# Prompt's dilated attention: copies of turned blocks placed between the exponentials of the next unit, scores issued three units ahead

## The reference, cut to what matters

```python
s = jnp.einsum("znqhe,znkhe->znhqk", qb, kb).astype(jnp.float32) * scale
s = s - slopes[:, None, None] * (dist * dilation).astype(jnp.float32)
s = jnp.where(valid[None, :, None], s, NEG_INF)
m = jnp.max(s, axis=-1)
e = jnp.exp(s - m[..., None])
den = jnp.sum(e, axis=-1)
o = jnp.einsum("znhqk,znkhe->znqhe", e, vb.astype(jnp.float32))
# merge_groups, with M the largest m of the groups:
num = sum(o * jnp.exp(m - M)[..., None] for o, m, _ in parts)
den = sum(dn * jnp.exp(m - M) for _, m, dn in parts)
return num / den[..., None]
```

## Time and profile before

| | us |
|---|---|
| Median of 3 runs | 1567.02 (1566.27 to 1567.53) |
| The profiled execution's own time | 1569.71 |
| Span of the profiled execution | 1567.9 |
| Busy in the span: TensorE / VectorE / GpSimd / ScalarE | 1461.7 / 673.4 / 612.9 / 467.1 |
| First instruction of the stage (line 1043) | at 1068.69 |
| First output-projection product (line 539) | at 1154.34 |

### The profile page before, as it was taken

The page is one execution under the profiler, slowest core; times in us unless marked ns, Lnnn a source line. Parts: engine busy times, 40 slices in busy tenths (PEclk is TensorE's granted clock), DMA queues, the critical chain, the costliest instruction groups (busy, mean ns, idle before and its releaser), DMA issues.

```text
span 1567.9 us, 28214 instructions
## 1 busy us (share of the span) xinstructions
PE 1461.7 (93%) x12103; PEld 1354.0 (86%) x12103; DVE 673.4 (43%) x984; ACT 467.1 (30%) x866; POOL 612.9 (39%) x276
## 2 busy tenths in 40 slices
PE   6969995888999999999999999998879999999998
PEld 6857763555899999999999999887669999999998
DVE  4668776777254400233113454425665420034212
ACT  4215544343332221122322111114633221122322
POOL 1412213342336644466343443231024654366441
PEclk9979997999999999999999999999989999999999
DMA  4234854675243544454433674558923444544421
GB/s 158 76 101 164 296 172 178 243 280 211 84 162 135 194 155 138 154 190 142 154 141 102 215 250 134 171 187 267 315 90 135 144 151 143 205 134 144 151 81 55
DMA packets 124060, 258.80 MB, mean 165 GB/s; under 512 B 7257, under 2 KB 104681, under 8 KB 117697
## 3 DMA queue, kind: packets, MB, share of 16 engines
q1 hardware_dynamic: 117824, 219.73, 41.1%
q0 software_dynamic: 6144, 37.75, 6.5%
HBM read 249.87 MB, written 95.58 MB: 220 GB/s over the span
## 4 chain that ended last, share of the span: by engine, by line
PE 86%; DVE 8%; issue 2%; ACT 2%; another core or an unknown queue 0%; DMA 0%; SPq 0%; POOL 0%; DVEq 0%; ACTq 0%
PE ps L539 23%; PE ps L543 23%; PE ps L540 22%; PE ps L846 4%; PE ps L748 2%; PE ps L867 1%; ACT sc L2276 1%; DVE KT L1566 1%; PE ps L795 1%; PE ps L1051 1%; PE ps L763 1%; PE ps L1085 1%; PE ps L952 1%; PE ps L887 1%; PE ps L728 1%
## 5 line engine op out<-in xcount | busy, mean ns | idle before, releaser
L2328 POOL TENSOR_TENSOR whl<-wraw,whl 128x2048 fp32r<-128x2048 f32 (+3 forms) x127 | 448.6, 3541 | 539.0 <-ACT whl L1975 539.0
L539 PE MATMUL ps<-hA,whl 128*128 128x260 f32 x1216 | 323.4, 287 | 11.1 <-POOL hA L2328 6.0
L540 PE MATMUL ps<-hA,whl 128*128 128x260 f32 x1216 | 318.6, 283 | 0.0
L1975 ACT ACTIVATE whl<-wraw 128x2048 fp32r<-128x2048 f32 (+3 forms) x127 | 186.1, 1486 | 424.6 <-PE ps L543 397.4
L539 PE MATMUL ps<-uT,whl 128*128 128x260 f32 x1024 | 268.4, 283 | 0.0
L540 PE MATMUL ps<-uT,whl 128*128 128x260 f32 x1024 | 266.3, 281 | 0.0
L543 PE MATMUL ps<-hA,whl 128*128 128x260 f32 x1216 | 247.4, 285 | 0.0
L539 PEld LDWEIGHTS ps<-hA,whl 128*128 128x128 f32 x1216 | 231.5, 190 | 14.5 <-issue 12.8
L540 PEld LDWEIGHTS ps<-hA,whl 128*128 128x128 f32 x1216 | 232.0, 191 | 0.1
L543 PE MATMUL ps<-uT,whl 128*128 128x260 f32 x1024 | 206.7, 283 | 0.0
L540 PEld LDWEIGHTS ps<-uT,whl 128*128 128x128 f32 x1024 | 193.2, 189 | 0.0
(11 more groups left out here) (303 smaller groups left out, 1991.9 us busy)
## 6 DMA issues: line engine op xcount, KB each, us to landing
out_ds<-in_state SPq DMA_DIRECT2D x32, 2047.0 KB, 10.4
wraw<-in_w_up SPq DMA_DIRECT2D x32, 1024.0 KB, 5.6
wraw<-in_w_down SPq DMA_DIRECT2D x32, 1024.0 KB, 5.1
wraw<-in_w_qkv SPq DMA_DIRECT2D x18, 1024.0 KB, 5.2
out_ds<-in_state SPq DMA_DIRECT2D x8, 2044.0 KB, 12.3
dv<-in_state SPq DMA_DIRECT2D x36, 256.0 KB, 5.3
dv<-q_scratch SPq DMA_DIRECT2D x6, 1024.0 KB, 6.2
wraw<-in_w_omla SPq DMA_DIRECT2D x4, 1024.0 KB, 11.2
```

Of the source, the lines that this page charges most:

```text
L539: pe.matmul(ps[:, 2 * u + a, 0:HALF], hi(k), rhs(k, 0)[:, c], start=first, stop=False)
L540: pe.matmul(ps[:, 2 * u + a, 0:HALF], hi(k), rhs(k, 1)[:, c], start=False, stop=False)
L1975: ins = act.activation(dst(0), src, ACT.Copy)
L2328: return pool.tensor_tensor(dst, src, hi.bitcast(F32), ALU.subtract)
```

## The change

ScalarE's loop runs one unit longer, and a copy of unit k - 1 follows each quarter of exponentials of unit k. TensorE issues the scores of units 0 to 2 first and then those of unit k + 3 after the second quarter's values of unit k; it also issues the turn of the maxima in unit 6 and the turn of the sums in the first quarter of unit 7, each behind a new wait. VectorE takes the result of a unit out one iteration later. No instruction is added or removed.

```diff
-            d_scores(0)
+            for k in range(3):
+                d_scores(k)
             for k in range(DU):
-                if k + 1 < DU:
-                    d_scores(k + 1)
                 d_turn(k, 0)
-                if k == DU - 1:
-                    for a in range(2):
-                        pe.wait_ge(dil_biased[a], DU)
-                    turn_stats(0, top)
                 for j in range(4):
                     if j < 3:
                         d_turn(k, j + 1)
-                    if k == DU - 1 and j == 2:
+                    if k == DU - 1 and j == 0:
+                        pe.wait_ge(dil_exp, 8 * DU)
                         turn_stats(1, total)
                     d_values(k, j)
+                    if j == 1 and k + 3 < DU:
+                        d_scores(k + 3)
+                    if j == 1 and k == DU - 2:
+                        pe.wait_ge(dil_max_ready, DU)
+                        turn_stats(0, top)
```

```diff
-            for k in range(DU + 2):
+            for k in range(DU + 3):
                 if k < DU:
                     d_max(k)
-                if k == DU + 1:
+                if k == DU + 2:
                     shares()
-                if k >= 2:
-                    d_out(k - 2)
+                if k >= 3:
+                    d_out(k - 3)
```

```diff
-            for k in range(DU):
+            for k in range(DU + 1):
                 for j in range(4):
-                    d_exp(k, j)
-                for j in range(4):
-                    d_taken(k, j)
-                    if k == DU - 1 and j == 2:
-                        share_exp()
+                    if k < DU:
+                        d_exp(k, j)
+                    if k:
+                        d_taken(k - 1, j)
+                if k == DU - 1:
+                    share_exp()
```

## The result

The changed kernel takes 1557.43 us (median of 4 runs, 1555.34 to 1559.50) against 1567.18 us: 9.75 us less, ratio 0.9937 with the 95% interval 0.9923 to 0.9950. The forecast was 1562.3 in a range of 1560.0 to 1566.3. The direction was right and the size was not: the change is worth twice what I said. Its profiled execution took 1557.15 us, with a span of 1555.3.

What follows compares the result with a forecast made beforehand. The stage was taken as bound by a ring of waits through TensorE, ScalarE and VectorE. Units 1 to 7 -7.2 us, tail +1.9, 0.6 taken back for hand-overs and clock: -4.7, median 1562.3, range 1560.0 to 1566.3.

Steps and rivals of the forecast that it cites:

- What bounds the stage: In the 76 us stage no engine is full; links waiting for one another across TensorE, ScalarE and VectorE set the time.
- The ring through three engines: VectorE's bias and maxima, ScalarE's exponentials and copy, TensorE's values and scores, then VectorE again: 17.35 us per pair, floor 14.8.
- the chain of the new order: Unit 1's first exponential to unit 7's, 46.05 us, then 14.3 to the first merge multiply (L1929).
- Even and odd iterations: Middle of the stage, new order: 8.9 us with kind 1 scores, 6.9 with kind 0, so 15.8 a pair against 17.35.
- the one without scores: Iteration 5, which issues no scores: ScalarE paces it, 5.95 us.
- The tail: From unit 7's first exponential to L1929: 14.3 us, 1.9 longer than the 12.4 before, since unit 6's copies are in it.
- The waits behind the new order: VectorE's work stays hidden: slack 1.6 us for scores, 0.5 to 2.6 for exponentials, cost 0 for results taken out later.
- the signs that I had named: Units 1 and 7 46 us apart, pairs 15.8, TensorE over 85% busy, L1929 about 1142.5, clock 1.00 from unit 1 to 6.
- how long the ring takes: Old order, from the first profile: 17.35 us a pair, 53.24 from unit 1's first exponential to unit 7's.
- C: Rival: short pauses drop TensorE's clock to 1.2 GHz in units 5 to 7, costing 7.4 us, giving 1569.7; chance 0.06.
- B: Rival: VectorE late once or twice, or a half-clock stretch stays; gain 2.9 us, 1564.1, down to none; chance 0.13.
- D: Rival: gain given back after the stage, where the projection waits for other engines; late clock costs 1 us; 1566.5; chance 0.05.

Runs made afterwards that it cites:

- warm_start: Changed kernel plus 10 extra identity products in each of TensorE's two waits at the stage's start; ratio 0.9943 to the kernel before.
- scores_two_ahead: Changed kernel with scores issued two units ahead in place of three; 1593.71 us, ratio 1.0145 to the kernel before.
- filler_products: Kernel before plus 7 or 4 extra identity products in TensorE's wait for the first copy of each unit; 1562.14 against 1567.96 us.
- before_again: Kernel before, unedited, profiled and timed once more; ratio 0.9998 to the runs beside it.
- after_again: Changed kernel, unedited, profiled and timed once more; 1559.45 against 1568.25 us for the kernel before, ratio 0.9944.
- after_third: Changed kernel, unedited, run again beside its variants; 1563.41 against 1572.46 us for the kernel before, ratio 0.9943.

## Why the prediction was wrong

- **What bounds the stage**: half of it. The ring through three engines did cost, and the chain of the new order came out at 60.34 us against 60.35 summed; that the clock cost about as much was missed (below). Even and odd iterations took 8.95 and 6.82 us, forecast 8.9 and 6.9; the one without scores 5.88, forecast 5.95. The first took 9.6, not 8.5: the clock had fallen while TensorE waited for VectorE ahead of the scores of unit 2, which then took 3.36 us. I had those scores down at 1.8 us; in warm_start, where they took 1.79, the first iteration is 8.48 us. The tail made up for it, 13.3 instead of 14.3, with the spreads at full clock (1.24 us for half of them instead of 2.07). That these two cancel to 0.01 us is luck: with the clock at 1.00 at the start the same stretch is 59.2 us.
- **The waits behind the new order**: right. The exponentials of units 2 to 7 wait for no maxima in the trace after, and scores_two_ahead shows what happens when they do. Of the signs that I had named, the pairs came as foretold (6.82 + 8.95 = 15.8 us) and TensorE was busy for 87% of the stage; the clock was below 1.00 until 1079, and the first merge multiply stood at 1136.51 and not at 1142.5, mostly because this execution came to unit 1 at 1076.2 and not at 1081.9.
- **The step that failed** is the one in which I said how long the ring takes: "three pairs, one of them dearer by the half clock", 53.24 us, and with it the 12.4 us of the way out: read from one execution and taken as the kernel's own. Over units 1 to 7 and the tail the next two profiles needed 68.9 and 68.8 us, not 65.6. The missed term is up to 3.3 us there, and its cause is shown by filler_products: the gaps of nearly 2 us that the change removes also pull the clock down, more often than the first profile had it.
- **The clock as a rival and not as a gain**: wrong in sign. I asked whether the new order might lower the clock (C, 0.06) and took 0.6 us back for late hand-overs and the way out, and never asked what the old order paid. The earlier trace rows held a warning: two equal gaps, of 1.79 us each, one with a drop behind it and one without, so a drop can't be counted on to come or to stay away; before_again then had one behind both. With drops after both of these gaps and at unit 7 the clock costs 5.0 us; with the order's own 3.6 this gives 8.6, and the measured differences are 9.75, 8.8 and 9.0 us. Part of that agreement is chance: 8.6 comes from executions 1.4 to 1.5 us slower than the median, and the times also hold the stretch behind the merge (below). With the clock at 1.00 in both orders the difference is 63.9 - 59.2 = 4.7 us, which is what the reordering saves by itself; the remaining 3.9 are the 5.0 before less the 1.1 that the changed kernel still loses.
- The Trainium skill's rule on TensorE that idles briefly between groups ("TensorE: Matmul & The Clock Gate", section "A second HAM failure mode: psum-queue depth-cycling") didn't come true in the changed kernel: with TensorE waiting 0.2 to 0.6 us at a time, the clock stayed at 1.00 for 56 us (after_again, 1084 to 1140). The kernel before did swing between the two clocks, but behind gaps of 1.79 us.
- **The second wrong assumption** was that the profiled execution's time and its stage go together. The first profile ran 2.7 us above the median although its stage was short, because it had come to unit 1 3.6 us later than before_again.
- **Rivals**: C didn't happen: the kernel after shows a clock of 1.00 from 1080 to 1140, units 5 to 7 included. Of B only a stretch at half clock was there, in the first iteration (1.1 us). D named something real and put it on the wrong side. From the merge to the end the profiles have two lengths, 418.8 to 418.9 us or 420.3 to 420.7, and the granted clock tells them apart in all 14. Each has a stretch at 1.2 GHz behind the merge. In the four short ones (after, after_again, filler_products, scores_two_ahead) it ends 10 to 11 us behind the merge, as the projection gets going, and TensorE has no other while it works. In the ten long ones it lasts until 15 or 16 us behind the merge, or another comes later, as at 1551 in after_third. The rows below are from before_again, after_again and after_third, in this order; the first two are at the same place, some 13 us behind the merge. Before and changed kernels have both lengths between them, so whether the change makes the short one more frequent isn't shown.

```profile
1160.00:1162.00 2.00, 2.00 (x11) 2.00 (x11) 0.70 (x1) 0.40 (x1) 0.00 (x0) 0.50 0.00 0
```

```profile
1152.00:1154.00 2.00, 2.00 (x19) 2.00 (x19) 0.61 (x2) 1.26 (x2) 0.00 (x0) 1.00 0.00 0
```

```profile
1551.00:1553.00 2.00, 2.00 (x11) 2.00 (x11) 0.85 (x5) 0.21 (x1) 0.00 (x0) 0.50 0.00 0
```

What stays open: what decides in an execution whether the clock falls there, and why the pages take 139 or 146 us. Both are in code that no edit touched. Whether 9.75 in the first job and 8.8 and 9.0 in the others differ at all can't be told, the intervals overlap.

## What to carry to other kernels

Where TensorE waits 1.5 to 2 us in a loop, price the wait twice: its own length, and the steps behind it at half clock; here the two were about equal (4.7 us for the order, 3.9 for the clock, of 8.6 from unit 1 to the merge). A few useless products in the gap measure that share in one run, before anything is reordered. A chain worked out from row prices can be right to 1 us and the forecast still be off by half, if the time that it is held against comes from a single execution: look in that profile for rows where the same pattern runs at two speeds.

## What the runs showed of the hardware

- Filling TensorE's gaps with products of the identity made a kernel 5.8 us faster (1562.14 against 1567.96 us).
- ScalarE alternated between exponentials and copies some 55 times with no table load between them and no price for the change of function: copy to exponential 0.47 to 0.50 us, exponential to exponential 0.49 to 0.51 (kernel after, 1076 to 1124).
- With TensorE busy 3.42 us of 4 in short bursts (1118 to 1122 in the kernel after) the granted clock stayed 1.00.
- A gap of 1.79 us in a busy stretch was followed by a granted clock of 0.50 in one place and not in another of the same execution (kernel before, 1103.83 and 1122.40).
- The same 420 us behind the merge took 1.5 to 1.9 us more in the ten profiles with a longer or a second stretch at 0.50 than in the four without.
